# A hybrid attention trunk on one core: where the factors of q and the last heads' splits stand in each engine's order

## The reference

```python
def rms_norm(x, gain):
    y = xf * lax.rsqrt(jnp.mean(xf * xf, axis=-1, keepdims=True) + NORM_EPS)
    return (y * gain.astype(jnp.float32)).astype(x.dtype)
...
    a_q, a_k, a_v, b_ql, b_kvl, b_kr = split_cols(h @ w_in, AB_IN_SPLITS)
    a_q = rope(rms_norm(a_q.reshape(B, S, 2 * A_HEADS, A_QK_DIM), a_q_norm), pos)
    a_k = rope(rms_norm(a_k.reshape(B, S, 2 * A_HEADS, A_QK_DIM), a_k_norm), pos)
...
    out_a = differential_attention(a_q[:, :, :, 0], a_q[:, :, :, 1], a_k[:, :, :, 0], a_k[:, :, :, 1],
                                   a_v, lam, A_QK_DIM ** -0.5)
    q_b = (rms_norm(b_ql, b_q_a_norm) @ b_w_q_b).reshape(B, S, B_HEADS, B_NOPE_DIM + B_ROPE_DIM)
...
    out_b = latent_attention(q_nope, q_rope, k_nope, k_rope, b_v,
                             (B_NOPE_DIM + B_ROPE_DIM) ** -0.5)
    mixed = jnp.concatenate([out_a.reshape(B, S, A_HEADS * A_V_DIM),
                             out_b.reshape(B, S, B_HEADS * B_V_DIM)], axis=-1)
    return mixed @ w_out
```

## Time and profile before

| what | value |
| --- | --- |
| median of 3 runs | 1268.74 us (1267.94 to 1269.54) |
| the profiled execution, its own time | 1269.42 us |
| its span, first to last instruction | 1267.0 us, 2.4 us less than its time |
| PE busy | 1243.5 us, 98% of the span |
| DVE, ACT, POOL busy | 45%, 47%, 43% |
| POOL's four steps for the factor of q1 (L433 to L439) | 164.37 to 165.49 us, 1.1 us |
| latent and first wide head, stretch 60 to 180 us | PE busy 111.64 of 120 us |

### The profile page before, as it was taken

How to read it: one execution, slowest core, us unless ns; L and a number is a source line. 1 busy time by engine, 2 the same in 40 slices (tenths; PEclk the granted TensorE clock), 3 DMA queues, 4 the chain that set the end, 5 groups by cost and what they waited for, 6 DMA issues and landing times.

```text
span 1267.0 us, 16841 instructions
## 1 busy us (share of the span) xinstructions
PE 1243.5 (98%) x6244; PEld 1053.1 (83%) x6244; DVE 566.4 (45%) x975; ACT 592.4 (47%) x979; POOL 550.4 (43%) x283
## 2 busy tenths in 40 slices
PE   9999989999999999999989999999999999999999
PEld 8899878788888888888878888887888888888887
DVE  8756687642221022221288888886322210122210
ACT  5779776543322122233377788884433221222320
POOL 4577821364454344456332222223644453344542
PEclk9999999999999999999999999999999999999999
DMA  6221111223232223332221112111323332232331
GB/s 212 86 67 51 50 34 34 63 84 117 99 123 94 68 98 99 106 114 80 67 68 50 58 58 66 50 50 34 116 100 99 102 108 89 84 99 94 114 116 41
DMA packets 29349, 105.95 MB, mean 84 GB/s; under 512 B 3376, under 2 KB 3888, under 8 KB 29296
## 3 DMA queue, kind: packets, MB, share of 16 engines
q1 hardware_dynamic: 29152, 105.20, 25.3%
q10 hardware_dynamic: 144, 0.02, 0.0%
HBM read 103.11 MB, written 2.10 MB: 83 GB/s over the span
## 4 chain that ended last, share of the span: by engine, by line
PE 85%; DVE 8%; ACT 3%; issue 2%; POOL 1%; DMA 0%; SPq 0%; POOLq 0%; ACTq 0%
PE bank L348 23%; PE bank L349 23%; PE bank L352 23%; PE bank L1534 3%; PE bank L1565 2%; PE bank L1481 1%; PE bank L1386 1%; PE bank L374 1%; PE bank L1388 1%; PE bank L1387 1%; DVE cs_lo L1509 1%; PE bank L1058 1%; ACT pn L1106 1%; PE bank L969 1%; PE bank L971 1%
## 5 line engine op out<-in xcount | busy, mean ns | idle before, releaser
L337 POOL TENSOR_TENSOR w_lo<-wraw,w_hi 128x1024 fp32r<-128x1024 f32 (+4 forms) x180 | 456.7, 2538 | 653.7 <-ACT w_hi L325 653.6
L348 PE MATMUL bank<-h_hi,w_hi 128*128 128x512 f32 x896 | 350.9, 392 | 0.1
L349 PE MATMUL bank<-h_lo,w_hi 128*128 128x512 f32 x896 | 349.0, 389 | 0.0
L325 ACT ACTIVATE w_hi<-wraw 128x1024 fp32r<-128x1024 f32 (+4 forms) x180 | 198.2, 1102 | 243.5 <-DVE x L673 125.6
L352 PE MATMUL bank<-h_hi,w_lo 128*128 128x512 f32 x896 | 221.8, 389 | 0.0
L348 PEld LDWEIGHTS bank<-h_hi,w_hi 128*128 128x128 f32 x896 | 168.2, 188 | 36.2 <-issue 1.1
L352 PEld LDWEIGHTS bank<-h_hi,w_lo 128*128 128x128 f32 x896 | 168.2, 188 | 34.9
L349 PEld LDWEIGHTS bank<-h_lo,w_hi 128*128 128x128 f32 x896 | 168.3, 188 | 34.3
L348 PE MATMUL bank<-f_hi,w_hi 128*128 128x512 f32 x352 | 136.9, 389 | 0.0
L349 PE MATMUL bank<-f_lo,w_hi 128*128 128x512 f32 x352 | 136.9, 389 | 0.0
L636 ACT ACTIVATE f_hi<-fa 128x512 f32 (+1 forms) x44 | 27.8, 632 | 217.2 <-DVE fa L662 217.2
(11 more groups left out here) (285 smaller groups left out, 1985.4 us busy)
## 6 DMA issues: line engine op xcount, KB each, us to landing
wraw<-in_w_in SPq DMA_DIRECT2D x120, 512.0 KB, 3.3
wraw<-in_w_down SPq DMA_DIRECT2D x32, 704.0 KB, 4.1
wraw<-in_w_ab SPq DMA_DIRECT2D x20, 512.0 KB, 3.4
x<-in_xt SPq DMA_DIRECT2D x8, 256.0 KB, 6.7
out<-x SPq DMA_DIRECT2D x8, 256.0 KB, 2.0
wraw<-in_w_ab SPq DMA_DIRECT2D x4, 416.0 KB, 6.8
wraw<-in_w_ab SPq DMA_DIRECT2D x2, 384.0 KB, 3.2
wraw<-in_w_ab SPq DMA_DIRECT2D x2, 256.0 KB, 2.8
```

The lines of the kernel that those rows point to most:

```text
L325: nc.scalar.activation(whi[:, s, at:at + width], wraw[:, s, at:at + width], ACT.Copy).then_inc(S("w_hi"), 1)
L337: nc.gpsimd.tensor_tensor(wlo[:, s, at:at + width], wraw[:, s, at:at + width], whi[:, s, at:at + width], ALU.subtract).then_inc(S("w_lo"), 1)
L348: nc.tensor.matmul(out_bank, w, src_hi[kt], start=(kt == 0), stop=False)
L349: nc.tensor.matmul(out_bank, w, src_lo[kt], start=False, stop=False)
```

## The change

It moves instructions and splits one group; none is added or removed.

1. POOL: `lo(11)` stands ahead of `b_pair_pool(pool, 0)`.
2. PE: two of the four steps `pj_pe(pe, 1, 1, i)` stand ahead of `b_qk_pe(pe, 0)`.
3. DVE: the low part of a head's output moves from the end of head u + 1 to the middle of head u + 2, behind the reciprocals; the mean for a factor moves from ahead of the reciprocals to behind that.
4. The mean and ACT's root for q1 move from the end of head 6 to its middle, ahead of `b_qk`.
5. ACT in head 7 no longer makes `mixed_hi` of head 6 and `w_hi` of chunk 21 ahead of the values' high part (`va_act`); they stand behind the last evacuation and behind block 1 of the first wide head.
6. DVE in the first wide head: maxima of blocks 0 and 1 first, then the additions and low parts.
7. PE in the first wide head: three of four tiles of `ob_pe(pe, 0, 0)` stand ahead of the scores of block 3.

```diff
@@ ob_pe
-    def ob_pe(pe, u, e):
+    def ob_pe(pe, u, e, tiles=range(4)):
...
+            if u == 0 and e == 0:
+                pe.wait_ge(S("h_mlo"), B_HEADS - 2)
+                pe.wait_ge(S("va_lo"), 2 * NB)
...
+        if u == 0 and e == 0 and tiles[-1] == 3:
             pe.wait_ge(S("h_mlo"), B_HEADS)
@@ gpsimd
+            lo(11)
             b_pair_pool(pool, 0)
-            lo(11)
             rs_newton_pool(pool, "b1", 48, Z_B[1])
@@ scalar, latent heads
-                if u in (1, 3, 5):
-                    rs_act(act, {1: "q0", 3: "k0", 5: "k1"}[u], 16)
+                if u in (1, 3, 5, 6):
+                    rs_act(act, {1: "q0", 3: "k0", 5: "k1", 6: "q1"}[u], 16)
...
-                if u:
+                if 0 < u < B_HEADS - 1:
                     b_mhi_act(act, u - 1)
-                hi_static(act, 14 + u)
-                if u == 6:
-                    rs_act(act, "q1", 16)
+                if u < B_HEADS - 1:
+                    hi_static(act, 14 + u)
...
             b_lower_act(act, B_HEADS - 1)
+            b_mhi_act(act, B_HEADS - 2)
@@ scalar, wide heads
+                a_exp_act(act, u, 1)
                 if u == 0:
                     b_mhi_act(act, B_HEADS - 1)
-                a_exp_act(act, u, 1)
+                    hi_static(act, 14 + B_HEADS - 1)
@@ vector, latent heads
-                if u in (1, 3, 5):
-                    qk_mean_dve(dve, {1: 0, 3: 2, 5: 3}[u])
                 b_inv_dve(dve, u, 0)
                 for c in range(1, 3):
                     b_inv_dve(dve, u, c)
+                if u >= 2:
+                    b_mlo_dve(dve, u - 2)
+                if u in (1, 3, 5, 6):
+                    qk_mean_dve(dve, {1: 0, 3: 2, 5: 3, 6: 1}[u])
...
-                if u:
-                    b_mlo_dve(dve, u - 1)
-                if u == 6:
-                    qk_mean_dve(dve, 1)
@@ vector, wide heads
+                a_max_dve(dve, u, 1)
                 if u == 0:
                     b_add_dve(dve, B_HEADS - 1)
-                a_max_dve(dve, u, 1)
-                if u == 0:
-                    b_mlo_dve(dve, B_HEADS - 1)
+                    b_mlo_dve(dve, B_HEADS - 2)
...
+                if u == 0:
+                    b_mlo_dve(dve, B_HEADS - 1)
                 a_max_dve(dve, u, 3)
@@ tensor
+            for i in range(2):
+                pj_pe(pe, 1, 1, i)
             b_qk_pe(pe, 0)
-            for i in range(NB):
+            for i in range(2, NB):
                 pj_pe(pe, 1, 1, i)
...
+                if u == 0:
+                    ob_pe(pe, u, 0, range(3))
                 a_scores_pe(pe, u, 3)
...
-                ob_pe(pe, u, 0)
+                ob_pe(pe, u, 0, range(3, 4) if u == 0 else range(4))
```

More of the change, by code:

```diff
@@ L1137, in b_lower_act @@
         act.wait_ge(S("h_o"), u + 1)
-        wait(act, "h_mlo", u - 1)
+        if u >= 2:
+            act.wait_ge(S("h_mlo"), u - 1)
         nc.scalar.activation(bo[b_rows(u), :], bank[OUT][B_V:P, :], ACT.Copy).then_inc(S("b_lower"), 1)
@@ L1388, in out_step_pe @@
         return nc.tensor.matmul(b, wlo[:, slot(g), w], mhi[:, first + k, :], start=False, stop=stop)
-    def ob_pe(pe, u, e):
+    def ob_pe(pe, u, e, tiles=range(4)):
         g = G_OB + u
-        pe.wait_ge(S("w_lo"), g + 1)
-        if u == 0 and e == 0:
+        if tiles[0] == 0:
+            pe.wait_ge(S("w_lo"), g + 1)
+            if u == 0 and e == 0:
+                pe.wait_ge(S("h_mlo"), B_HEADS - 2)
+                pe.wait_ge(S("va_lo"), 2 * NB)
+            else:
+                pe.wait_ge(S("ob_x"), 2 * u + e)
+        if u == 0 and e == 0 and tiles[-1] == 3:
             pe.wait_ge(S("h_mlo"), B_HEADS)
[L1395 to L1398, removed]
+        for k in tiles:
             last = out_step_pe(g, e, bank[7][:], k, A_HEADS, k == 0, k == 3)
-        last.then_inc(S("chunk_done" if e else "ob"), 1)
+        if tiles[-1] == 3:
+            last.then_inc(S("chunk_done" if e else "ob"), 1)
     def ob_dve(dve, u, e):
```

## The result

The changed kernel took 1271.13 us in the median of 19 runs (1269.69 to 1272.55), the kernel before 1268.40 in 19 runs beside it (1267.14 to 1270.87): ratio 1.0021, 95% interval 1.0014 to 1.0028. It is slower, by about 2.7 us in the medians. In the profiled executions 1271.08 stands against 1269.42, and the spans differ by 1.9 us.

What follows compares the result with a forecast made beforehand. PE, busy 98% of the span, bounds the kernel, so only its gaps or slow stretches matter. Terms -3.4 + 3.6 + 1.35 + 0.15 - 3.5 + 2.1 + 1.2 give +1.5 us: 1270.9 profiled, 1270.2 median, range 1268.3 to 1272.3.

Steps and rivals of the forecast that it cites:

- The start: Ahead of head 0's first score: POOL's earlier subtraction and PE's reordered products bring it to 67.6 from 71.01, minus 3.4 us.
- Heads 3, 5 and 6: Latent heads: moved DVE operations wait for POOL and delay ACT's root, plus 1.8 us each in 3 and 5, 1.35 in 6.
- the two take turns: Latent heads: DVE operations with both inputs in SBUF wait for POOL's whole operation in flight, the two engines alternating.
- The rival in which DVE keeps its turn: Latent heads: the mean follows the low part before POOL gets in; heads 3 and 5 cost nothing, 1265.6 us; chance 0.19.
- Head 1: Only the mean moves: 0.5 us late if POOL is first, 0.2 better if DVE is; taken as plus 0.15.
- Head 7: From its first score to the wide head: 10.9 us instead of 14.4, q1's factor no longer holding ACT; minus 3.5.
- The wide head to its transposes: First wide head: DVE's product and probabilities wait for POOL's moved operations, 2.8 less 0.7, plus 2.1 us.
- The 0.7 counted: First wide head: without POOL, the stretch to the transposes would end about 0.7 us earlier.
- The clock's fall: First wide head: PE's gap of about 5 us brings the clock to 0.50; at most 1.5 us, taken as plus 1.2.
- the slow stretch: Start of the kernel before: sixteen matmuls at half clock take 3.34 us instead of 1.8, costing 1.5 us.
- the slower rival: The clock still falls at the start, 1.5 us more, or the dear ends come: 1271.7 to 1272.5 us; chance 0.14.
- the two dear ends: Costlier outcomes of head 1 and the first wide head: 0.3 and 0.7 us more than forecast.

Runs made afterwards that it cites:

- the kernel with the mean first: The changed kernel with DVE's mean ahead of the low part of an output, both still behind the reciprocals: 1266.95 us, ratio 0.9982 to the kernel before.
- The early scaling: The changed kernel with POOL's Newton steps for q1 and scaling of k ahead of the subtraction for chunk 21: 1268.80 us, ratio 0.9993 to 1.0011 around 1.0002.
- the three kernels of the last group: Changed kernel with scaling early, chunk 21's high part later, and part 3 mostly undone, without or with sixteen filler matmuls, or mean first with filler: ratios 0.9947, 0.9943, 0.9955.
- The filler, whole and half: The changed kernel with 40 or 20 unread matmuls of 256 columns ahead of the first wide head's transposes: 1268.97 us (ratio 1.0005) and 1270.07 us (1.0010).

## Why the prediction was right, and where a term was off

The forecast was +1.5 us in the profiled execution, and +1.7 came (+2.05 between the marks of the table). It spoke of 1270.2 by the median, and 1271.13 was measured, inside its own range.

Against the kernel before in the same rounds it is less close: 1271.13 beside 1268.40 is +2.7 (1.8 to 3.6 by the interval), where +1.5 was forecast. The forecast was built on one profiled execution of the kernel before, in which the clock fell at the start. Of the 67 runs of that kernel beside the experiments 23 have a mean clock of 1.000, so no such fall; the 19 runs of the changed kernel have 0.997 (13) or 0.999 (6). So in about a third of its runs the kernel before has no fall to lose, while every run of the changed kernel has one somewhere, most of them as much as the profiled one. How much of the missing 1.2 us this makes was not measured.

- **The start** was right as a term: -3.49 for -3.4, transposes at 63.89 for 64.0, no clock of 0.50 ahead of the first score. What the prediction did not see is that a fall avoided here can come back elsewhere: the kernel with only this part lost 0.62 of it in the first wide head. Part of the hit is luck. The ten kernels with the new start stand at 67.38 to 68.76, in the middle at 68.0, which would be -3.0; and the kernel with DVE's new order alone, whose start is the old one, had its first score at 69.31 where the clock stayed up, 1.7 us ahead of the 71.01. PE's gap ahead of the transposes was 0.14 us by the rows, not 0.7.
- **Heads 3, 5 and 6** were right in place, mechanism and size: +1.72, +1.72 and +1.26 for 1.8, 1.8 and 1.35. The low part lasts 1.16 us, of which it waits 0.60 for L1010, L1028 lasts 2.25 and ends with L1012, and PE waits for `pt_lo`, 1.3 us rather than the 1.5 or more that I named. The rule of the Trainium skill ("SBUF — State Buffer", Who interferes with whom), that a VectorE instruction with two SBUF inputs and a GpSimd one that reads SBUF exclude each other, agrees with all of it: a mean over 16 elements ends 0.03 us behind POOL's L1012. That the two take turns, as the prediction read it, was wrong as a rule, as the kernel with the mean first showed: who is taken up first goes first. The rival in which DVE keeps its turn is true in that order (heads of 10.7 us), and untrue in this one.
- **Head 1** was left open between two cases, and the cheap one came: the mean was taken up at 82.40 us, POOL's L1012 at 82.41, and the mean lasted 0.18. -0.15 for +0.15. It was no matter of chance: in all seven traces with this order DVE is first, by 0.01 to 0.03 us, and the head takes 10.68 or 10.69.
- **Head 7** was right: -3.58 for -3.5, and no wait ahead of its transposes. Parts 4 and 5 were not run alone; DVE's new order alone already gave 2.4 of the 3.6.
- **The wide head to its transposes**: +1.76 for +2.1. The product waited 0.7 (0.8 forecast), the probabilities 1.6 (1.9). The early scaling, which takes the second of these away, shortened this stretch, from 13.71 to 12.0 us (160.92 to 172.91). The 0.7 counted was near, too: without any meeting, in the three kernels of the last group, the stretch took 11.34, 0.61 less than the 11.95 before. What the prediction didn't name is that before, the product of block 1 already met the scaling of k and waited about 0.75 us for it, so that the old order had a meeting of its own to lose; whether the 0.61 is that one or the output matmuls, no run tells apart. DVE's row in the kernel before:

```profile
166.46 0.91 DVE L1244 SCALAR_TENSOR_TENSOR tiny<-tiny 128x2 f32<-128x2 f32 x1
```

- **The clock's fall** came where it was forecast, and its term was the one mis-sized: "The price is at most the 1.5 of the start" gave +1.2, and 2.8 was measured. The 1.5 was taken from a stretch of 3.41 us; behind a gap of 5.11 it lasted 6.83. The filler, whole and half, shows both steps: 2.8 for the long one, 1.5 for the short one. The prediction's other remark, that part of it may lie in the gap, is borne out: from its transposes to the second wide head the head takes 5.84 us with the clock up, and with 6.83 us of low clock 8.62, 8.39 and 8.01 where the stretch began 0.9, 1.4 and 2.1 us ahead of the transposes (the changed kernel, the early scaling, the mean first).

The slips of the other terms (-0.09, -0.16, -0.09, -0.30, -0.08, -0.34) add up to -1.06 and hid most of the clock's 1.6. That the sum came so near was luck. Two counts in the prediction are off without bearing on it: the matmuls from 63.92 to 67.26 are fifteen, not sixteen, so the slow stretch cost 1.6 by that working (the two traces with the old start, one with the fall and one without, differ by 1.5 from the end of the gap to the first score); and in the slower rival the two dear ends alone give 1271.2, and all three together 1272.7.

Why the low stretch is once 3.41 and once 6.83 us long is only in part answered. Behind gaps of 2.71 and 2.74 us it was 3.41, behind 3.40, 5.08, 5.09 and 5.11 it was 6.83, but each of these is one profiled execution of one kernel, and the runs' mean clocks show that it differs between executions: among the 11 runs with the early scaling the three whose mean clock was 1.000 took 1267.2 to 1267.5 us, and the two with 0.997 took 1269.9 and 1270.6.

## What to carry to other kernels

Before a VectorE operation with two SBUF inputs is moved onto a path that other engines wait for, look at which GpSimd operation is in flight there, and at what stands just ahead of it: put the short operation on which others wait first, and the long one behind it (here 1.7 us a head). An idle stretch of PE has to be priced twice, once as itself and once by the clock behind it, and where neighbouring stretches are marginal, a fall avoided in one may only move to the next. When a sum comes out right, check its terms: here errors of opposite sign made it so. And where the clock falls in some executions and not in others, one profile of the kernel before is one case of several: look at the mean clocks of the runs too.

## What the runs showed of the hardware

- Between two engines that exclude each other, the operation taken up first went first, even by 0.01 to 0.03 us (head 1 in seven traces, heads 3 and 5 with the mean first).
- The clock's low stretches last 3.41 or 6.83 us, the second twice the first; nothing between was seen in this part of the kernel.
- The same gaps don't always bring the clock down. The kernel with DVE's new order alone has the start of the kernel before. PE's timeline and a window of it:

```profile
61.48 0.61 PE L1165 MATMUL bank<-mat,qb 128*96 128x128 f32 x4 [0.92 <-issue]
63.74 0.39 PE L969 MATMUL bank<-w_hi,h_hi 128*128 128x256 f32 x1 [1.20 <-POOL w_lo L337]
...
64.00:66.00 2.00, 2.00 (x19) 2.00 (x19) 0.25 (x1) 0.00 (x0) 1.82 (x4) 1.00 0.65 182
```

  Gaps of 0.92 and 1.20 us as in the earlier trace rows, and a clock of 1.00 where the earlier trace rows has 0.50. In this execution it fell at 167.60 instead, and once more at 662.54, far behind the change, for 3.41 us each. Behind the first wide head's two waits for exponentials (0.75 and about 1.3 us) it fell in this kernel and in the one with the new start alone, and not in the kernel before.
- POOL's memsets don't hold DVE up. In head 7 of the changed kernel the low part, taken up during one memset and running on beside the next, lasted 0.69 us, as long as in the first wide head with POOL idle (163.41, 0.69):

```profile
153.17 0.69 DVE L1155 TENSOR_TENSOR mixed_lo<-bo,mixed_hi 64x512 fp32r<-64x512 f32 x1
...
152.78 0.52 POOL L1340 MEMSET aq_lo<- 64x512 f32 x1
153.36 0.52 POOL L1342 MEMSET aq_lo<- 64x512 f32 x1
```
